# One decoder layer with 32 experts: a shorter routing ahead of the first gather, the rest of it inside the expert steps

## What is computed

```
n  = rmsnorm(x);  p = n @ w_in                    # q1 q2 | k1 k2 | v | B C h
a  = diff_attention(p, bias table, past keys and values)   # 4 heads, two softmax maps of 64 columns a head
c  = short gated convolution of the B, C, h columns
h  = x + [a || c] @ w_out
m  = rmsnorm(h);  group = argmax(m @ w_group) of 4;  two best of the 8 experts in that group
y  = h + gate * sum over the two of gate_e * (silu(m @ gate_e) * (m @ up_e)) @ down_e   # 32 experts, d_ff 256
out = rmsnorm(y)
```

## Time and profile before

| | us |
|---|---|
| median of three runs | 1072.74 (1069.87 to 1073.26) |
| the profiled execution | 1070.95 |
| its span in the trace | 1069.1 |
| mean granted clock of PE | 0.94 |

### The profile page before, as it was taken

How to read it: one execution, slowest core, us unless ns; L and a number is a source line. 1 busy time by engine, 2 the same in 40 slices (tenths; PEclk the granted TensorE clock), 3 DMA queues, 4 the chain that set the end, 5 groups by cost and what they waited for, 6 DMA issues and landing times.

```text
span 1069.1 us, 14098 instructions
## 1 busy us (share of the span) xinstructions
PE 916.2 (86%) x4937; PEld 749.7 (70%) x4937; DVE 577.2 (54%) x1032; ACT 499.4 (47%) x830; POOL 442.3 (41%) x332
## 2 busy tenths in 40 slices
PE   4899999999999999958969997289999999999700
PEld 3799887888788778845757665178888887777500
DVE  4504532353325332767645137787777767767347
ACT  4423344334433434253312121558888877777412
POOL 1102322222332323223313120078999975565475
PEclk9999999999999999979979998589999999999955
DMA  8033223232121103270253521989999999998785
GB/s 263 18 93 101 80 80 94 88 99 80 41 62 30 51 28 103 86 236 1 83 168 119 177 84 64 360 311 376 410 412 406 413 405 399 402 397 329 280 283 204
DMA packets 92554, 206.25 MB, mean 193 GB/s; under 512 B 12767, under 2 KB 54303, under 8 KB 84294
## 3 DMA queue, kind: packets, MB, share of 16 engines
q1 hardware_dynamic: 79950, 168.13, 43.3%
q10 hardware_dynamic: 5528, 20.04, 4.8%
q0 software_dynamic: 7008, 17.18, 4.5%
HBM read 171.19 MB, written 42.34 MB: 200 GB/s over the span
## 4 chain that ended last, share of the span: by engine, by line
PE 66%; DVE 10%; DMA 9%; issue 5%; POOL 4%; ACT 4%; SPq 2%; ACTq 0%; POOLq 0%; DVEq 0%
PE pj L971 25%; PE pj L1854 11%; PE pj L1060 7%; DMA e_raw<-in_w_up 7%; PE pj L1900 6%; PE pj L1037 5%; PE pj L1022 3%; POOL f_y L2112 2%; PE tp L1829 2%; PE tp L1011 1%; DVE e_lo L1806 1%; DVE sc L1253 1%; DMA k_page<-in_cache_k 1%; PE pj L1452 1%; PE tp L994 1%
## 5 line engine op out<-in xcount | busy, mean ns | idle before, releaser
L971 PE MATMUL pj<-n_hi,w_hi 128*128 128x350 f32 (+1 forms) x576 | 200.3, 348 | 3.4 <-DVE n_lo L1291 3.4
L1806 POOL TENSOR_TENSOR e_lo<-e_raw,e_hid 128x2048 fp32r<-128x2048 f32 x32 | 167.6, 5237 | 72.8 <-ACT e_hid L1802 72.7
L971 PE MATMUL pj<-n_lo,w_hi 128*128 128x350 f32 (+1 forms) x576 | 188.4, 327 | 0.0
L971 PE MATMUL pj<-n_hi,w_lo 128*128 128x350 f32 (+1 forms) x576 | 187.5, 325 | 0.0
L1806 DVE TENSOR_TENSOR e_lo<-e_raw,e_hig 128x2048 fp32r<-128x2048 f32 x64 | 148.6, 2324 | 0.1
L669 POOL TENSOR_TENSOR w_lo<-w_raw,w_hi 128x1024 fp32r<-128x1024 f32 x21 | 50.1, 2388 | 204.5 <-ACT w_hi L744 204.5
L1802 ACT ACTIVATE e_hig<-e_raw 128x2048 fp32r<-128x2048 f32 x64 | 122.7, 1919 | 25.3 <-DMA e_raw<-in_w_up 18.7
L971 PEld LDWEIGHTS pj<-n_hi,w_hi 128*128 128x128 f32 x576 | 109.7, 190 | 32.3 <-issue 30.4
L1253 DVE CUSTOM_DVE_ANT_0 sc<-pj,strip 128x512 f32<-128x512 f32 (+5 forms) x120 | 61.6, 545 | 102.1 <-PE pj L1037 60.6
L971 PEld LDWEIGHTS pj<-n_lo,w_hi 128*128 128x128 f32 x576 | 110.0, 191 | 0.6
L971 PEld LDWEIGHTS pj<-n_hi,w_lo 128*128 128x128 f32 x576 | 109.8, 191 | 0.7 <-issue 0.6
(11 more groups left out here) (257 smaller groups left out, 1710.8 us busy)
## 6 DMA issues: line engine op xcount, KB each, us to landing
...
```

The lines of the kernel that those rows point to most:

```text
L971: ins = pe.matmul(pj[g % 2][:, 0:tn], ws[w][:, P * k:P * (k + 1)], x[:, k, t0:t0 + tn], start=(m == 0), stop=(m == 23))
L1806: eng.tensor_tensor(e_lo[r][:, q, :], e_raw[r][:, q, :], e_hi(par, q).bitcast(F32), ALU.subtract).then_inc(s_lo[q], 1)
```

## The change

- The first slot list has 32 blocks only. `route_place` no longer subtracts whole blocks: a rank above 128 matches no place. It is split in `route_rank` and `route_place`; for tiles 0 to 6 the first runs ahead of the last tile's normed rows and the second right behind them. Tiles 7 and 8 go through `route_top2`, `route_rank` and `route_place` together, and PE adds 14 of the slot products before their marks are there, 4 after.
- A maximum's index is found by a code (95 minus the index) in four operations instead of five. The mask takes two operations instead of three. The token table is written tile by tile in `tokens`.
- What further blocks need (their count, list, rows, the addresses of the results and the gates) is done by `route_more` on DVE in the steps 0 to 13, `pe_more` on PE in the steps 7, 9 and 11 and `act_gates` on ACT in step 1.
- SP loads experts 0 and 1 in slot 51, expert 2 ahead of the last logits and expert 3 right behind them. ACT writes the high parts of expert 0 in slot 54. The zero fill of the gather's buffer on ACT is left out. Buffers are placed anew for it, those of the last stage also.
- POOL's low part is four instructions of 512 columns.
- A score pair waits once for both banks, and has up to twelve fillers behind it instead of six.

```diff
+                if s == S_BACK + 1:
+                    sp.wait_ge(s_be, USE[("z", 0, 0)] + 1)
+                    for q in (1, 0, 2):
+                        load_piece(sp, 0, q, 0, 0, 0)
+                    sp.wait_ge(s_dm, MIXN[(NT - 1, 0)] + 1)
+                    for q in (1, 0, 2):
+                        load_piece(sp, 1, q, 1, 0, 1)
...
+                if s == S_BACK + 4:
+                    act.wait_ge(s_csl, 2 * NT)
+                    for q in (1, 0, 2):
+                        high(act, 0, q, 0, 0)
...
+            u = PIE[s] + 2 * p
+            if u >= 2:
+                pe.wait_ge(s_sb, u)
             for c in range(2):
-                u = PIE[s] + 2 * p + c
-                if u >= 2:
-                    pe.wait_ge(s_sb, u - 1)
...
                         pe_qk(pe, s, p)
-                        fill(ga, 6)
+                        fill(ga, 12)
...
+                    if i == NT - 1:
+                        route_rank(dve, did, 0, TE)
                     dve.wait_ge(s_hrstd, i + 1)
...
                     dve.scalar_tensor_tensor(hn[0:M, i % 2, :], h_sb[0:M, i % 2, :], hst[0:M, i % 2, 2:3], g_ffn[0:M, :], ALU.mult, ALU.mult).then_inc(s_hn, 1)
+                    if i == NT - 1:
+                        route_place(dve, did, 0, TE)
...
                     route_top2(dve, did, 5, TE)
-                if s == S_EARLY + 1:
-                    route_place(dve, did, 0, TE)
...
 
 
         RD = 4
-        e_raw = [at(f"e_raw{r}", [P, 3, 2048], F32, r0 + (24576 * r if r < 3 else 83456)) for r in range(RD)]
-        e_lo = [at(f"e_lo{r}", [P, 3, 2048], F32R, r0 + (24576 * r if r < 3 else 83456)) for r in range(RD)]
+        e_at = [r0 + 83456, r0, r0 + 24576, r0 + 49152]
+        e_raw = [at(f"e_raw{r}", [P, 3, 2048], F32, e_at[r]) for r in range(RD)]
+        e_lo = [at(f"e_lo{r}", [P, 3, 2048], F32R, e_at[r]) for r in range(RD)]
...
+            def first_max(vals, n, m, v, tmp):
 
                 do(dve.tensor_reduce(m, vals, AX.X, ALU.max))
                 do(dve.tensor_tensor(tmp, vals, each(m, T, n), ALU.is_equal))
-                do(dve.scalar_tensor_tensor(tmp, tmp, -64.0, over_rows(iota32, T, n), ALU.mult, ALU.add))
-                do(dve.tensor_reduce(idx, tmp, AX.X, ALU.min))
-                do(dve.tensor_scalar(idx, idx, 64.0, None, ALU.add))
+                do(dve.tensor_tensor(tmp, tmp, over_rows(code, T, n), ALU.mult))
+                do(dve.tensor_reduce(v, tmp, AX.X, ALU.max))
 
             if t0 == 0:
+                dve.wait_ge(s_csl, MIXN[(NT - 1, 0)] + 1)
+                dve.wait_ge(s_wol, 8)
                 did(dve.memset(mark[:].bitcast(F32), 0.0))
-                did(dve.memset(nxs[:, :, 0:NE], 0.0))
...
-            x1 = dve.tensor_tensor(grp[:, 1, t0:t1], g, each(gs[:, 0, t0:t1], T, NG), ALU.subtract)
-            x1.then_inc(s_rx, 1)
-            do(dve.tensor_tensor(eq[:, t0:t1], over_rows(C("iotag"), T, NE), each(gs[:, 1, t0:t1], T, NE), ALU.is_equal))
-            do(dve.tensor_scalar(eq[:, t0:t1], eq[:, t0:t1], -1.0, BIG, ALU.add, ALU.mult))
-            do(dve.tensor_tensor(lem[:, t0:t1], eq[:, t0:t1], e, ALU.add))
+            dve.tensor_tensor(grp[:, 1, t0:t1], g, each(gs[:, 0, t0:t1], T, NG), ALU.subtract).then_inc(s_rx, 1)
+            do(dve.tensor_tensor(eq[:, t0:t1], over_rows(C("codeg"), T, NE), each(gs[:, 1, t0:t1], T, NE), ALU.not_equal))
+            do(dve.scalar_tensor_tensor(lem[:, t0:t1], eq[:, t0:t1], -BIG, e, ALU.mult, ALU.add))
...
-            do(dve.tensor_tensor(eq[:, t0:t1], hot2[:, 0, t0:t1], hot2[:, 1, t0:t1], ALU.add))
-            dve.tensor_tensor(mark[:, 1 + t0:1 + t1, :], eq[:, t0:t1], each(C("valid")[:, t0:t1], T, NE), ALU.mult).then_inc(s_mark, 1)
+            if t1 == NT:
+                do(dve.tensor_tensor(eq[:, t0:t1], hot2[:, 0, t0:t1], hot2[:, 1, t0:t1], ALU.add))
+                dve.tensor_tensor(mark[:, 1 + t0:1 + t1, :], eq[:, t0:t1], each(C("valid")[:, t0:t1], T, NE), ALU.mult).then_inc(s_mark, 1)
+            else:
+                dve.tensor_tensor(mark[:, 1 + t0:1 + t1, :], hot2[:, 0, t0:t1], hot2[:, 1, t0:t1], ALU.add).then_inc(s_mark, 1)
             dve.tensor_tensor(gs[:, 2, t0:t1], ms[:, 1, t0:t1], ms[:, 0, t0:t1], ALU.subtract).then_inc(s_rx, 1)
-
...
+        def tokens(dve, did, t0, t1):
+
+            T = t1 - t0
+            dve.wait_ge(s_step, did.n[0])
+            for c in range(2):
+                did(dve.tensor_tensor(block_tok[:, c, t0:t1], hot2[:, c, t0:t1], each(C("token1")[:, t0:t1], T, NE), ALU.mult))
+
+        def route_rank(dve, did, t0, t1):
+
             T = t1 - t0
             dve.wait_ge(s_rank, 1 if t0 == 0 else 2)
             for c in range(2):
...
+            did(dve.tensor_reduce(rk[:, 0, :, t0:t1], big2[:, :, t0:t1], AX.X, ALU.add))
+
...
+            dve.wait_ge(s_step, did.n[0])
             for c in range(2):
...
-            do(dve.scalar_tensor_tensor(rk[:, 3, :, t0:t1], rk[:, 2, :, t0:t1], -float(P), rk[:, 0, :, t0:t1], ALU.mult, ALU.add))
-            for c in range(2):
-                dve.tensor_tensor(place_hot[:, c, t0:t1], over_rows(C("iota128"), T, P), each(rk[:, 3, c, t0:t1], T, P), ALU.is_equal).then_inc(s_ph, 1)
+                dve.tensor_tensor(place_hot[:, c, t0:t1], over_rows(C("iota128"), T, P), each(rk[:, 0, c, t0:t1], T, P), ALU.is_equal).then_inc(s_ph, 1)
...
+            route_rank(dve, did, TE, NT)
             route_place(dve, did, TE, NT)
-            ov = C("over")
-            over_e = big2[:, 0, 0:8, :].rearrange("p a b -> p (a b)").rearrange("p (e j) -> p e j", j=8)
+            do(dve.tensor_copy(cnt[:], rank_ps[:, NT, :]))
+            dve.wait_ge(s_pm, 1)
+            do(dve.tensor_scalar(slot_f[:], pj[1][:, 0:NE], 0.0, 4096.0, ALU.is_equal, ALU.mult))
+            do(dve.scalar_tensor_tensor(slot_f[:], pj[1][:, 0:NE], -1.0, slot_f[:], ALU.add, ALU.add))
+            do(dve.tensor_copy(slot_tok[:, 0:NE], slot_f[:]))
+            dve.sem_inc(s_slots, 1)
+
+        def route_more(dve, did, n):
...
-            do(dve.tensor_scalar(slot_f[:], pj[1][:, 0:MAXB], 0.0, 4096.0, ALU.is_equal, ALU.mult))
-            do(dve.scalar_tensor_tensor(slot_f[:], pj[1][:, 0:MAXB], -1.0, slot_f[:], ALU.add, ALU.add))
-            did(dve.tensor_copy(slot_tok[:], slot_f[:]))
...
+            if n == 0:
+                did(dve.memset(nxs[:, :, 0:NE], 0.0))
+                do(dve.tensor_tensor(over_e[:], spread(cnt[:], [[1, NE], [0, 8]]), over_rows(C("over"), NE, 8), ALU.is_gt))
+                do(dve.tensor_reduce(nx[0], over_e[:], AX.X, ALU.add))
+            elif n == 1:
+                for i, d in enumerate((1, 2, 4, 8, 16)):
+                    do(dve.tensor_tensor(nx[(i + 1) % 2], nx[i % 2], nxs[:, i % 2, NE - d:2 * NE - d], ALU.add))
+            elif n in (2, 3):
+                c = n - 2
+                do(dve.tensor_tensor(big_x[:], hot2[:, c], over_rows(below, NT, NE), ALU.mult))
+                do(dve.tensor_reduce(rk[:, 1, c], big_x[:], AX.X, ALU.add))
...
+            elif n in (6, 8, 10):
+                for j in (n - 6, n - 5):
+                    c, t0 = j // 3, 3 * (j % 3)
+                    if j >= 2:
+                        dve.wait_ge(s_pm, j)
+                    dve.tensor_tensor(place_x[:, j % 2], over_rows(C("iota128"), 3, P), each(rk[:, 3, c, t0:t0 + 3], 3, P), ALU.is_equal).then_inc(s_ph, 1)
+            elif n == 7:
+                do(dve.scalar_tensor_tensor(flat[6], flat[3], float(MAXB), flat[5], ALU.mult, ALU.add))
+                did(dve.tensor_copy(addr[:], flat[6]))
...
+            elif n == 12:
+                dve.wait_ge(s_pm, 7)
+                do(dve.tensor_scalar(slot_x[:], pj[2][:, 0:XB], 0.0, 4096.0, ALU.is_equal, ALU.mult))
+                do(dve.scalar_tensor_tensor(slot_x[:], pj[2][:, 0:XB], -1.0, slot_x[:], ALU.add, ALU.add))
+                did(dve.tensor_copy(slot_tok[:, NE:MAXB], slot_x[:]))
+            elif n == 13:
+                dve.wait_ge(s_re, 4)
...
         def act_r(act):
-            act.wait_ge(s_rx, 5)
-            act.activation(grp[:, 2], grp[:, 1], ACT.Exp).then_inc(s_re, 1)
-            for q in (1, 0, 2):
-                high(act, 0, q, 0, 0)
-            act.wait_ge(s_rx, 6)
-            act.activation(gs[:, 4, :], gs[:, 2, :], ACT.Exp).then_inc(s_re, 1)
-            for w in range(2):
-                act.wait_ge(s_hst[w], 16 * (5 - w))
-                act.wait_ge(s_hnst[w], 16 * (5 - w))
-            act.activation(xg[:], spread(C("ones"), [[0, RD * D // P], [1, P]]), ACT.Copy, scale=0.0).then_inc(s_re, 1)
+            act.wait_ge(s_hx, 2 * NT)
+            act.wait_ge(s_dm, 2 * NT)
             for q in (1, 0, 2):
                 high(act, 1, q, 1, 1)
+
+        def act_gates(act):
+            act.wait_ge(s_rx, 6)
+            act.activation(grp[:, 2], grp[:, 1], ACT.Exp).then_inc(s_re, 1)
+            act.activation(gs[:, 4, :], gs[:, 2, :], ACT.Exp).then_inc(s_re, 1)
...
+            pe.wait_ge(s_t, 2 * NT)
+            for c in range(2):
```

(43 more changed lines are left out.)

195 lines of the change are left out of this document (96 added, 99 removed).

## The result

The changed kernel takes 1082.24 us in the median of four runs (1081.19 to 1082.52), the kernel before 1071.45 (now four runs, 1069.87 to 1073.26). The ratio is 1.0096, with a 95% interval of 1.0076 to 1.0115: 10.8 us slower, where 9.8 faster was forecast.

A forecast was written before the change was run, and what follows sets the result against it. PE was taken to bound attention and early expert steps, DMA transfers the late ones. Attention -3.3, routing to the first gather -7.5 and expert steps +1.0 gave -9.8 on 1072.74: 1063 us, range 1053 to 1075 (8 in 10).

The forecast's parts named there:

- Attention, -3.3: Score pairs and fillers in attention: fewer PE stalls, 1.1 us a head in heads 0 to 2, -3.3 us in all.
- Routing up to the first gather: From the routing chain to the first gather: issue 12.5 us earlier, but only -7.5 us credited after landing under load.
- the 1.2 + 0.7 ahead of them: DVE routing before the last marks: 1.2 us from moving place_hot, 0.7 from a shorter first routing of tiles 0 to 4.
- The gather under load: First gather's landing amid expert loads: the loaded 10.0 us median taken instead of the unloaded 4.56, landing at 689.
- T0: SP's first load issue after an expert's gate and up products, at 707.77 before; the expert stage follows it one to one.
- the bigger gain: Rival at the first gather: it shares engines with the loads, landing near 685.3; -13.5 us, about 1057; chance 0.16.
- Expert steps, +1.0: Expert stage: a longer load lead against added routing, PE products and table loads; +1.0 us, bounds -1 and +6.
- at nothing: POOL's low part in four, expert steps: +0.6 us on POOL, hidden beside a DMA-bound 10 us step, so no cost.
- DVE has 2.5 us free in one: Expert steps: DVE's idle time takes about 1 us of routing a step; cost 0.1 a step, 1.2 in all.
- the two table loads: ACT in step 1: two exponentials add two loads of 1.28 us; cost put at 0 to 2.6.
- PE's added products: Expert steps: three times six products of 16 columns, 1.3 us each time; up to 3.9, taken at 0.3.
- The slower one: Rival in the expert steps: DVE and POOL become the bound, 10.6 us a step; +19, near 1091; chance 0.10.

The follow-up runs named there:

- e10: Kernel before with only the new score pairs (one wait for both banks, up to twelve fillers): 1067.67 us, ratio 0.9965.
- e2: Kernel before with only POOL's low part split into four instructions of 512 columns, no routing moved: 1082.69 us, ratio 1.0088.
- e9: Changed kernel with POOL's low part in quarters only in steps 0 to 13, one instruction from step 14 on: 1074.78 us, ratio 1.0035.
- e5: Changed kernel with POOL waiting on its own previous quarter before each next one: 1080.44 us, ratio 1.0069.

## Why the prediction was wrong

**Attention, -3.3: right.** The store at 656.12 came at 653.24, -2.9, and e10 gives -4.1 by its times. The pairs did what was forecast, on PE of the changed kernel:

```profile
228.63 0.49 PE L1056 MATMUL pj<-kT,qT 64*128 64x128 f32 x4 [0.55 <-DVE ust L1272]
...
252.57 0.92 PE L1056 MATMUL pj<-kT,qT 64*128 64x384 f32 x4
```

The second halves no longer wait (0.49 and 0.92 us for 1.10 and 1.32). Of the fifth tile's wait of 0.91 us only 0.36 went, where I had credited all. In e10 the store came at 651.67, 4.5 us earlier and 1.6 before the changed kernel's, so another part of the change may cost something ahead of it; one execution each can't tell.

**Routing up to the first gather: about right in sum, one term off.** The gather issues at 677.85, 14.1 us earlier than the earlier trace rows; 2.9 of it are the attention's, so -11.2 for a forecast of -12.5. The top-2 took 4.72 us after 5.55 (-0.83 for -0.95), and from the marks to the gather it is 4.93 us for a forecast of 5.0. What fell short is the 1.2 + 0.7 ahead of them: only 0.6 came. The changed kernel's PE shows why:

```profile
666.82 1.12 PE L1212 MATMUL pj<-router,hnT 128*24 128x36 f32 x16 [1.53 <-DVE logits L1394]
```

The last router product waits for the copy of the logits of the tile before, which now stands behind place_hot. I had named what is queued behind place_hot on DVE only for the last tile.

**The gather under load: right.** 8.8 us for a forecast of about 9.5. T0 is -9.6 for -10.8. The rule of the Trainium skill, DMA: Bandwidth & Descriptors (Queues, rings and completion order), weighed as the bigger gain, would have it near the unloaded 4.7; the runs show that a queue of its own did not spare the gather 4.1 us. They don't contradict the turns between queues, only what I made of them.

**Expert steps, +1.0: wrong, +23.6 in the 27 steps and -2.5 behind them.** Two steps of the working failed, both on the same ground: they took busy time for room. The first is "at nothing" for POOL's low part in four: I had its price right (4.94 to 5.04 us unhindered, forecast 5.15) and rightly saw POOL's idle 0.65 to 0.8 us, but took a DMA-bound step of 10 us as cover, while the steps to the nineteenth are PE's and are full on the shared access. Alone this is +13.8 in the 27 steps and +10.6 in the time (e2). The second is "DVE has 2.5 us free in one": free by busy time, not by access. A routing operation costs not its own 0.2 to 1 us but the rest of POOL's instruction. The other 9.8 us of the +23.6 are this and its interplay with the quarters, which no run takes apart: e9, with quarters only where the routing is, has 266.14, 9.5 over before; 7.2 us are steps 5 to 7 and 6.3 one burst, and against them stands that its late steps are 9.3 or 9.4 us and not 9.7 to 10.6. Of the other items of that paragraph the two table loads left steps 0 and 1 at 9.2 and 9.3 us, 18.5 together after 17.7. PE's added products, taken at 0.3 in all, were mis-sized: they make the steps 7 and 11 10.0 us long and are 0.81 of step 9, some 2 us for the three (my estimate), inside the bound of 3.9.

**The rival.** The slower one named the mechanism, DVE and POOL excluding each other, its place and the point from which it decides (a mean step of 9.91 us). The mean was 280.23 / 27 = 10.38, for its 10.6. It had a chance of 0.10. Its cost was still too high, +19 for +10.8. What should have raised it stood in its own sum: 10.8 us for a step that lasts 9.36 already. I dismissed it with POOL's share of busy time, though POOL's 5.46 us in the median against 4.57 at the least showed that POOL spent 0.9 us of most instructions waiting. The Trainium skill, GPSIMD Engine Reference (8. Key points), names contention with DVE instructions with two SBUF inputs or in a two-port mode. The trace agrees for the first kind; the cast with one input, 1.20 us instead of 0.18, would fit the second, though no trace shows its mode.

**Not settled.** Why a burst recurs after seven or eight steps was only argued (0.45 us of lag a step). Who gets the shared access when both want it wasn't tried. In the kernel before, DVE's second low part starts at 807.76 while a gather still runs to 808.40, and takes its 2.28 us; in the burst it starts at 788.90 beside a gather in the same way, 0.66 us ahead of POOL's first quarter, and yet waits for all four. The visible difference is that POOL's next instruction follows the gather at once (0.03 us) instead of after 0.63. In e5, with a gap between the quarters, DVE waits less, but the steps gain nothing.
